# RWKV scan kernel on one Trainium2 core: the identity and R matmuls of a scan's states, issued in groups ahead of the products that are added to them

## The reference, cut to what matters

```
def step(S, inp):
    r_t, w_t, kk_t, a_t, k_t, v_t = inp
    sa = einsum('bhvk,bhk->bhv', S, -kk_t)
    S = (S * w_t[:, :, None, :] + sa[..., None] * (kk_t * a_t)[:, :, None, :]
         + v_t[..., None] * k_t[:, :, None, :])
    return S, einsum('bhvk,bhk->bhv', S, r_t)
```

## Time and profile before

| | |
|---|---|
| median of 3 runs | 2974.27 us (2972.38, 2974.27, 2994.22) |
| the profiled execution's own time | 2993.71 us |
| its span in the trace | 2991.9 us |
| PE busy | 2815.9 us, 94% of the span |
| DVE, ACT, POOL busy | 39%, 21%, 6% |
| share of PE in the chain that ended last | 87% |
| mean granted clock of PE | 0.96 |

### The profile page before, as it was taken

One profiled execution on the slowest core, in us unless ns is written; L12 is line 12 of the kernel. 1 busy time (PEld: TensorE's weight loads), 2 busy tenths in 40 slices (PEclk: granted clock), 3 DMA queues, 4 the chain that ended last, 5 costly groups with the idle time before them and its releaser, 6 DMA issues.

```text
span 2991.9 us, 58184 instructions
## 1 busy us (share of the span) xinstructions
PE 2815.9 (94%) x26080; PEld 1754.3 (59%) x26080; DVE 1168.7 (39%) x1938; ACT 627.6 (21%) x1182; POOL 169.5 (6%) x201
## 2 busy tenths in 40 slices
PE   6999998999999999999999999988999989999999
PEld 3555754566666666555545557545756666665555
DVE  2453625734435262111134535357354443522111
ACT  3111124322313131100021111243222231320000
POOL 0010000010101000000000100000101010100000
PEclk8999999989899899999999999999999998999999
DMA  6111120100000010121341111201000100001212
GB/s 246 49 46 57 57 98 8 44 10 30 18 24 24 17 31 10 57 99 58 130 149 44 51 57 54 94 15 37 18 29 12 36 11 23 24 24 57 99 58 69
DMA packets 40208, 155.13 MB, mean 52 GB/s; under 512 B 4992, under 2 KB 4992, under 8 KB 38944
## 3 DMA queue, kind: packets, MB, share of 16 engines
q1 hardware_dynamic: 35856, 131.09, 13.4%
q0 software_dynamic: 4112, 20.39, 1.8%
HBM read 144.64 MB, written 6.82 MB: 51 GB/s over the span
## 4 chain that ended last, share of the span: by engine, by line
PE 87%; DVE 7%; ACT 2%; issue 2%; DMA 1%; POOL 0%; DVEq 0%; PEld 0%; SPq 0%; ACTq 0%; POOLq 0%
PE ps L556 85%; DVE scr L1844 1%; DVE scr L1866 1%; PE ps L1006 1%; DVE scr L1857 1%; DVE scr L1991 0%; DMA ring<-in_w 0%; DVE scr L1856 0%; PE ps L841 0%; ACT scr L1573 0%; DMA cst<-in_cst 0%; PE ps L978 0%; DVE scr L1979 0%; DVE scr L1669 0%; ACT scr L1313 0%
## 5 line engine op out<-in xcount | busy, mean ns | idle before, releaser
L556 PE MATMUL ps<-h,ring 128*128 128x512 f32 (+1 forms) x4480 | 1266.0, 439 | 16.0 <-ACT h L1304 11.3
L556 PEld LDWEIGHTS ps<-h,ring 128*128 128x128 f32 x4480 | 695.6, 192 | 577.1 <-issue 571.4
L556 PE MATMUL ps<-scr 32*32 32x32 f32 (+9 forms) x17704 | 782.3, 229 | 78.6 <-issue 25.8
L556 PEld LDWEIGHTS ps<-scr 32*32 32x32 f32 (+5 forms) x17704 | 570.3, 124 | 272.7 <-issue 207.9
L556 PE MATMUL ps<-scr,cst 64*64 64x128 f32 (+2 forms) x544 | 166.2, 416 | 9.4 <-ACT scr L1508 9.4
L2085 DVE SCALAR_TENSOR_TENSOR scr<-scr,ps 128x640 f32<-128x640 f32 x32 | 26.3, 821 | 323.9 <-PE ps L556 323.5
L556 PE MATMUL ps<-scr,ring 128*128 128x512 f32 (+1 forms) x512 | 143.6, 442 | 4.0 <-DVEq L2090 4.0
L556 PEld LDWEIGHTS ps<-scr,cst 128*128 128x128 f32 (+1 forms) x544 | 77.2, 179 | 73.7 <-issue 71.1
L556 PEld LDWEIGHTS ps<-scr,ring 128*128 128x128 f32 x512 | 79.5, 194 | 67.9 <-issue 63.5
L1597 ACT ACTIVATE scr<-ps 128x640 f32<-128x640 f32 x32 | 22.5, 703 | 433.2 <-PE ps L556 433.2
L2007 DVE COPY_PREDICATED scr<-cst,ps 128x80 f32<-128x80 int32 x128 | 32.1, 251 | 173.6 <-PE ps L556 172.9
(11 more groups left out here) (262 smaller groups left out, 2298.5 us busy)
## 6 DMA issues: line engine op xcount, KB each, us to landing
ring<-in_w SPq DMA_DIRECT2D x240, 512.0 KB, 3.5
x<-in_x SPq DMA_DIRECT2D x1, 2560.0 KB, 16.2
yc<-in_win POOLq DMA_DIRECT2D x2, 1280.0 KB, 8.6
x<-in_x POOLq DMA_DIRECT2D x1, 2560.0 KB, 9.6
out_y<-x POOLq DMA_DIRECT2D x8, 320.0 KB, 6.2
x<-out_y POOLq DMA_DIRECT2D x1, 2560.0 KB, 10.4
out_y<-x SPq DMA_DIRECT2D x8, 320.0 KB, 3.4
scr<-in_inv POOLq DMA_DIRECT2D x2, 1152.0 KB, 5.5
```

Source lines behind the costliest of these rows:

```text
L556: return nc.tensor.matmul(out, lhsT, rhs, start=start, stop=stop)
```

## The change

In place of `transition` and `reader`, which put the 64-row matmul and the 128-row product of each head one behind the other, there are two functions for each bank: `states_begun(half)` issues all the 64-row matmuls of the bank (identities, then R), and `states_joined(half)` issues all the 128-row products that are added to them. The number of matmuls, their operands and the regions that they write stay the same. For the second bank `states_of_u(3, order[3])` now comes behind `states_joined(1)`, which increments `PT_full`, instead of ahead of it. The first matmul of a bank in each half of the partitions carries the start flag, where before each region's first matmul did.

```diff
-                        def transition(n, c):
-                            at = transition_in(states_bank(half_of(n)), n)
-                            for hh, hr in heads_of_tile:
-                                mm(at[hr], ident[hr, hr], ident[hr, hr], True, False)
-                                mm(at[hr], u_part(c, hh, 1), head_cols(Btok, c, hh), False, True)
-
-                        def reader(n, c):
-
-                            at = reader_in(states_bank(half_of(n)), n)
-                            for hh, hr in heads_of_tile:
-                                mm(at[hr], ident[hr, hr], AR[hr, c * 256 + 128:(c + 1) * 256], True, False)
-                                i = mm(at[hr], u_part(c, hh, 1), ABQ[hh][:, c * 256 + 128:(c + 1) * 256], False, True)
-                            return i
+                        def states_begun(half):
+
+                            at = states_bank(half)
+                            for n in (1, 2) if half == 0 else (3,):
+                                for hh, hr in heads_of_tile:
+                                    mm(transition_in(at, n)[hr], ident[hr, hr], ident[hr, hr], n != 2, False)
+                            for n in (1, 2) if half == 0 else (3, 4):
+                                c = order[n]
+                                for hh, hr in heads_of_tile:
+                                    mm(reader_in(at, n)[hr], ident[hr, hr], AR[hr, c * 256 + 128:(c + 1) * 256], False, False)
+
+                        def states_joined(half):
+                            at = states_bank(half)
+                            for n in (1, 2) if half == 0 else (3,):
+                                c = order[n]
+                                for hh, hr in heads_of_tile:
+                                    mm(transition_in(at, n)[hr], u_part(c, hh, 1), head_cols(Btok, c, hh), False, False)
+                            last = 2 + 2 * half
+                            for n in (last - 1, last):
+                                c = order[n]
+                                for hh, hr in heads_of_tile:
+                                    i = mm(reader_in(at, n)[hr], u_part(c, hh, 1), ABQ[hh][:, c * 256 + 128:(c + 1) * 256], False, n == last)
+                            i.then_inc(PT_full, 1)
...
-                        for n in (1, 2):
-                            transition(n, order[n])
-                        for n in (1, 2):
-                            i = reader(n, order[n])
-                        i.then_inc(PT_full, 1)
+                        states_begun(0)
+                        states_joined(0)
                         for n in (1, 2):
                             states_of_u(n, order[n])
                         pe.wait_ge(Ub_ready, 2 * g + 1)
+                        states_begun(1)
+                        states_joined(1)
                         states_of_u(3, order[3])
-                        transition(3, order[3])
-                        for n in (3, 4):
-                            i = reader(n, order[n])
-                        i.then_inc(PT_full, 1)
```

## The result

The changed kernel takes 2854.04 us (median of 4 runs, 2852.33 to 2857.36), the kernel before 2980.52 us (4 runs, 2972.38 to 2994.22): a ratio of 0.957, with a 95% interval of 0.953 to 0.961. The forecast was 2848, its range 2822 to 2886.

A forecast was written before the change was run, and what follows sets the result against it. PE was taken to bound the kernel, busy 94% of the span. Grouping (93.6 us) and the restored clock (51.8 us) sum to 145.4 us off the profiled 2993.71, giving 2848.3 us; range 2822 to 2886.

The forecast's parts named there:

- The grouped stretch: First identity to end of last reader: 9.05 us falls to 3.2 at full clock, 93.6 us over sixteen scans.
- Who could be late: Copies by ACT and DVE that PE needs: none late; ACT's first-bank copy done by 2.4 us, 1.3 us slack.
- The clock: In the nine scans at low clock, it stays at 1.00 once the couples are gone: 9 x 5.75 = 51.8 us.
- the first rival: In the scans, the clock falls all the same: 15 to 52 us, so 2864 to 2900 us; chance 0.08.
- The second: Pairs don't overlap where products join sums begun earlier: 2890 us with the clock's gain, 2942 without; chance 0.05.
- The third: 64-row pairs of identities and R take turns at their bank: 18 us more in all, 2867 us; chance 0.03.
- The fourth: Products wait for earlier writes in a bank under one start flag: 60 us slower, 3054 us; chance 0.02.
- falls elsewhere: The clock falling in work that now follows sooner on a scan's end would make the predicted size wrong; no size given.
- the median run of before: With 3.4 fewer low-clock scans than profiled, it saves less and ends at the same 2848 us; otherwise at 2829.

The follow-up runs named there:

- head-by-head run: The changed kernel with each bank made for head 0 alone (its 64-row matmuls, then products), then for head 1: 2902.34 us, ratio 0.974.
- pairs-only run: The kernel before, with each transition and reader issuing both heads' 64-row matmuls, then both products; row counts still alternate: 2874.95 us, ratio 0.963.
- the first bank alternating: The changed kernel with its first bank alternated head by head as before and the second bank grouped: 2926.90 us, ratio 0.983.
- the second trace of each kernel: The kernel before, unchanged, traced once more: 2997.08 us; the changed kernel run once more: 2852.46 us, ratio 0.955.
- both banks first: The changed kernel with the 64-row matmuls of both banks issued ahead of all products: 2848.07 us, ratio 0.955; run again, 2849.17 us, ratio 0.954.
- heads one behind the other: The changed kernel with all matmuls of head 0 ahead of head 1's inside each group, groups kept: 2866.72 us, ratio 0.961.

## Why the prediction was right

**The grouped stretch** (forecast 3.2 us, the moved `states_of_u(3)` counted in; measured 1107.98 - 1104.79 = 3.19, and each group above within 0.03 us): right, and for the reason given. The scan at full clock went from 12.47 to 6.66, 5.81 us where 5.85 was forecast. Two runs separate its parts: pairing gives 4.33 (to 8.14), the longer groups 1.48. Pairing itself has two parts. The head-by-head run gives up the overlap of the heads and has four changes of row count more, for 2.99 us; less four pauses of 0.152, some 2.4 us are the overlap (an estimate), and the other 1.9 of the 4.33 are the pauses that pairing saves. The pause is no wait of a product for the identity beneath it: the even beat of 0.256 us in the earlier trace rows has it ahead of every identity, too.

**Who could be late** was right as well: ACT's copy of the first bank (L1584) is done 1107.04 - 1104.79 = 2.25 us after the first identity, forecast 2.4, and among PE's waits in this trace there is none for it or for L2056.

**The clock** (forecast 9 x 5.75 us): right. It is 1.00 in all sixteen stretches, so the first rival is out, and the nine low scans give back their 5.75 each. What brought it down was put too simply, though. I named PE's pause at every matmul; the pairs-only run pauses thirteen times in its stretch and the head-by-head run has no overlap at all, and neither falls. In the kernels traced here the clock fell in this place only where both came together, lone matmuls with a pause ahead of each (the kernel before, and the first bank alternating). Why it takes both stays open.

**The rivals.** The second (products added to a sum don't pair) fails on the 1.05 us of the first bank's products, `states_of_u(1)` and `(2)` among them: the bank's eight products alone would need 4 x 0.104 + 4 x 0.208 = 1.25. The third (the 64-row pairs take turns at their bank) fails on the 0.82 us of the first group: taking turns would need 2 x 0.624 + 0.152 = 1.40. The fourth (waits under one start flag) fails on the 1.05 us as well, since twelve products at 0.33 to 0.43 us each would need over 4. The Trainium skill, TensorEngine Tiling (Array Packing), section Restrictions and Gotchas, says that different row tiles cannot access the same PSUM bank at the same time. Read as a rule that whole matmuls take turns, it does not agree with this trace (0.82 us, not 1.40) where the two tiles write different partitions.

**What was mis-sized.** The forecast held everything outside the scans constant. In the profiled executions the scans gave 7 x 12.47 + 9 x 18.2 - 16 x 6.66 = 144.5 us, as forecast (145.4), but the span lost only 136.3: the rest of the program grew by 8.2 us. With the 0.9 us by which the scans gave less, that is the 9.1 us between the 2848.3 forecast for the profiled execution and its 2857.36. The stretch between the seventh and the eighth scan, and the sum of all stretches outside the scans, before:

```profile
1134.35:1174.95 40.60, 36.30 (x1027) 1.00 0.06 17
...
sum 2740.86, PE 2564.89; mean PE 150.88
```

and after:

```profile
1062.18:1104.79 42.61, 38.89 (x1025) 0.92 0.06 17
...
sum 2749.05, PE 2570.30; mean PE 151.19
```

The work of this stretch is the same; the clock fell in it after the change and not before, and it is 2.0 us longer. Of the 17 stretches some grew and some shrank; 1.7 us came ahead of the first scan, where nothing was changed. I named falls elsewhere as what could make the size wrong. That they come more often because the change closes up the work is not shown. The rest varies from one execution to the next: the second trace of each kernel has 2995.3 - 256.9 = 2738.4 us before and 2849.8 - 16 x 6.66 = 2743.2 after, and "both banks first" has 2843.0 - 16 x 6.36 = 2741. Outside the scans the eleven traces of the changed kernel and its variants lie between 2741 and 2749 us, so a part of the growth may belong to the change; these runs don't separate it.

The forecast also needed the median run of before to save less and to end at the same time as the profiled one, which it called an estimate that no row bears out. The medians moved by 126.5 us, the profiled executions by 136.4, and the two ended within 3.4 us of each other. That fits, with the number of low scans in the runs without a trace still inferred from mean clocks.

## What to carry to other kernels

Where small matmuls of one PE stream use different rows and halves of the array, read their beat from the starts of the weight loads, at two sizes: what doesn't shrink with the columns is a pause at the change of shape, and a group with both heads that takes no longer than one head's half of it shows that the two overlap. Order the matmuls so that neighbours use the same number of rows and different halves of the partitions; most of the gain (4.3 of 5.8 us per scan here) needs only that two heads stand side by side. Look at the granted clock of such a stretch as well: here lone matmuls with pauses cost another 5.75 us in every scan in which the clock fell.

## What the runs showed of the hardware

PE works further ahead than the next matmul: with heads one behind the other, identities of head 1 started (625.53) ahead of R matmuls of head 0 (625.63, 625.74) that stand before them in the program, and half of the overlap survived (0.89 us lost per scan in place of 1.9). A change between 64 and 128 rows cost 0.15 us at full clock (ten changes 1.48 us, two 0.30). And the clock's fall in this place follows neither from the pauses nor from the lack of overlap alone: it stayed at 1.00 with thirteen pauses (pairs only) and without overlap (head by head, 6.4 us), and fell in half of the scans with 4.9 us of both.
